# Modulation weights in four column pieces, gate products later, and 24 units of the second block's weights split on chip

## What is computed

```python
mod = silu(c) @ ada_w + ada_b                      # 6 x 1024 numbers, ada_w is 1024 x 6144
sh1, sc1, g1, sh2, sc2, g2 = split(mod)
h = rmsnorm(x, norm1_g) * (1 + sc1) + sh1
z, xbc, dt, u_v = split(h @ w_in)                  # w_in 1024 x 4624
xbc = silu(causal_conv4(xbc)); y = ssd_chunked(xbc, dt) + d * xs      # chunks of 128 tokens
y = group_rmsnorm(y * silu(z)); g = rmsnorm(u * spatial_gate(v))
x = x + g1 * (concat(y, g) @ w_out)
h = rmsnorm(x, norm2_g) * (1 + sc2) + sh2
x = x + g2 * ((silu(conv3(h @ w_up_gate)) * (h @ w_up_val)) @ w_down)
return rmsnorm(x, final_g)
```

## Time and profile before

| | |
|---|---|
| runs | 2772.1, 2769.61, 2765.91 us |
| the profiled execution's own time | 2763.87 us |
| its span | 2762.1 us |
| TensorE busy | 2697.5 us, 98% of the span |
| VectorE, ScalarE, GpSimd busy | 1815.1, 1003.4, 1072.4 us |
| DMA | 616.29 MB, mean 223 GB/s |
| granted TensorE clock | nine tenths or more in each of 40 slices |

### The profile page before, as it was taken

The page is one execution under the profiler, slowest core; times in us unless marked ns, Lnnn a source line. Parts: engine busy times, 40 slices in busy tenths (PEclk is TensorE's granted clock), DMA queues, the critical chain, the costliest instruction groups (busy, mean ns, idle before and its releaser), DMA issues.

```text
span 2762.1 us, 33801 instructions
## 1 busy us (share of the span) xinstructions
PE 2697.5 (98%) x12427; PEld 2207.2 (80%) x12427; DVE 1815.1 (66%) x2544; ACT 1003.4 (36%) x1521; POOL 1072.4 (39%) x739
## 2 busy tenths in 40 slices
PE   7999999999999999999999999999999999999998
PEld 6777887787878888887878888888888788887886
DVE  6977956768287565568787565555746855455767
ACT  3543325321153333343535322152223433334333
POOL 3444435445057777654650100001102544444240
PEclk9999999999999999999999999999999999999999
DMA  9876877999846566483448767587676334445646
GB/s 383 281 268 246 313 263 248 349 328 315 287 129 218 201 207 217 157 293 96 148 160 298 236 211 280 177 284 235 210 261 201 117 116 127 126 125 207 217 167 221
DMA packets 261872, 616.29 MB, mean 223 GB/s; under 512 B 26597, under 2 KB 84425, under 8 KB 257611
## 3 DMA queue, kind: packets, MB, share of 16 engines
q1 hardware_dynamic: 261046, 613.89, 64.9%
...
## 4 chain that ended last, share of the span: by engine, by line
PE 82%; DVE 6%; DMA 5%; issue 3%; POOL 2%; SPq 1%; ACT 1%; DVEq 0%; ACTq 0%; POOLq 0%
PE main L2038 34%; PE pair L2310 15%; PE main L2310 14%; PE pair L2330 6%; PE main L2330 5%; DMA w_split_scratch<-w_hl 2%; PE pair L2179 2%; POOL w_hl L739 1%; PE pair L2204 1%; PE pair L2164 1%; PE pair L2171 1%; DVE a_lo L1659 1%; DMA ada_t<-in_ada_w_dram 1%; DMA w_hl<-w_split_scratch 1%; POOL tb L750 1%
## 5 line engine op out<-in xcount | busy, mean ns | idle before, releaser
L739 POOL TENSOR_TENSOR w_hl<-w_raw,w_hl 128x512 fp32r<-128x512 f32 x548 | 794.2, 1455 | 920.5 <-ACT w_hl L844 918.8
L844 ACT ACTIVATE w_hl<-w_raw 128x512 fp32r<-128x512 f32 x548 | 342.3, 630 | 831.9 <-PE main L2310 169.4
L2038 PE MATMUL main<-w_hl,h_hi 128*128 128x512 f32 x1536 | 493.4, 403 | 5.1 <-DMA w_hl<-w_split_scratch 2.8
L2038 PEld LDWEIGHTS main<-w_hl,h_hi 128*128 128x128 f32 x1536 | 285.9, 189 | 77.8 <-issue 14.7
L2038 PE MATMUL main<-w_hl,h_lo 128*128 128x512 f32 x768 | 301.3, 392 | 0.0
L781 POOL TENSOR_TENSOR pre_hl<-pre_raw,pre_hl 128x512 fp32r<-128x512 f32 x35 | 51.0, 1461 | 566.3 <-ACT pre_hl L868 566.3
L2038 PE MATMUL main<-h_hi,w_hl 128*128 128x512 f32 x768 | 247.7, 396 | 7.4 <-POOL w_hl L739 4.2
L750 POOL TENSOR_TENSOR tb<-tb,tb 128x512 f32<-128x512 f32 x132 | 198.1, 1501 | 113.9 <-DMA tb<-in_ff_up_dram 109.5
L2310 PE MATMUL pair<-s_hi,w_hl 128*128 128x512 f32 x736 | 235.8, 393 | 2.4 <-POOL w_hl L739 2.4
L2330 PE MATMUL main<-w_hl,a_hi 128*128 128x512 f32 x704 | 219.2, 393 | 7.3 <-DVE a_lo L1659 3.9
L1659 DVE TENSOR_TENSOR a_lo<-g,a_hi 128x512 fp32r<-128x512 f32 x132 | 160.8, 1226 | 96.6 <-ACT a_hi L1094 96.1
...
## 6 DMA issues: line engine op xcount, KB each, us to landing
...
w_split_scratch<-w_hl SPq DMA_DIRECT2D x104, 512.0 KB, 7.1
...
```

Of the source, the lines that this page charges most:

```text
L739: nc.gpsimd.tensor_tensor(w_lo[:, g % RING, :], w_raw[:, g % RING, :], w_hi[:, g % RING, :].bitcast(F32), ALU.subtract).then_inc(w_lo_ok, 1)
L844: nc.scalar.activation(w_hi[:, g % RING, :], w_raw[:, g % RING, :], ACT.Copy).then_inc(w_hi_ok, 1)
L2038: ins = T.matmul(main[i], a, w, start=first and p == 0, stop=last and p == 2)
```

## The change

It has three parts.

First, the start. The first 2048 columns of ada_w are loaded as four pieces. Each has all 1024 rows and 256 columns of sh1 and the same 256 of sc1, and is loaded by four transfers of 128 x 4 x 256 elements, so each contiguous run is 1 KB where it was 8 KB (or 4 KB twice). `DIRECT` = (4, 4, 0, 0): of pieces 0 and 1 rows 0 to 511 go to TensorE, all others to VectorE as sums of 2 x 256 elements, 24 in all. A piece gives the modulation of two row tiles of h. The column products of pieces 1, 2 and 3 stand behind units 0, 2 and 4. The weights of units 0 to 7 stand between the pieces in SyncE's order. The x tiles for h use three banks, and four h_lo (`HF0` = 4) are done by GpSimd. VectorE scales two of the four x tiles.

Second, the gates. The tiles of ada_w for the gates are loaded at units 8, 10, 13, 15, 18, 21, 24 and 27 (`GATE_AT`), their sums are spread over the convolutions and chunk 0, and their products (now 4 x 512 into one bank) stand behind the scores of chunk 1. Ahead of the product with the state of chunk 1, TensorE waits for `gate_ok`, which the 4-row addition on VectorE sets. The loads for sh2 and sc2 move (`COL_AT`).

Third, block 1. `RAW_TO` goes from 20 to 28, so that eight more units are loaded raw and split. The steps of the sums 0, 1 and 2 alternate with the low parts of units 16 to 27. `T_AT` places the loads of sums 0, 1, 2 at units 16, 20, 24 and of the others from 28 on, so the store of sum t comes directly ahead of the load of sum t + 1 there.

```diff
-        ADA_RING, ADA_FIRST, HF0, ADA_PE = 12, 8, 2, 2
+        PIECES, HF0, ADA_SEMS, DIRECT = 4, 4, 12, (4, 4, 0, 0)
+        PW = D // PIECES
...
-        GATE_TILES = {8: 12, 11: 13, 14: 14, 17: 15}
-        COL_AT = {20: 1, 28: 0, 40: 2, 48: 3, 56: 4, 68: 5, 78: 6, 84: 7}
+        GATE_AT = {8: 0, 10: 1, 13: 2, 15: 3, 18: 4, 21: 5, 24: 6, 27: 7}
+        COL_AT = {31: 0, 41: 1, 43: 2, 48: 3, 56: 4, 68: 5, 78: 6, 84: 7}
...
-        T_AT = ((), [16 + 17 * i // 5 for i in range(20)], [18 + 19 * i // 2 for i in range(13)])
+        T_AT = ((), [16, 20, 24] + [28 + 33 * i // 10 for i in range(17)], [18 + 19 * i // 2 for i in range(13)])
...
-        RAW_FROM, RAW_TO = RING, 20
+        RAW_FROM, RAW_TO = RING, 28
...
+            def piece_load(p, half):
+                rows_h = ada_w[0, 4 * half * P:(4 * half + 4) * P, :].rearrange("(k p) (s d) -> p k s d", p=P, d=D)
+                for part in range(2):
+                    sp.dma_start(ada_p[p][:, 4 * half:4 * half + 4, part, :], rows_h[:, :, part, p * PW:(p + 1) * PW]
+                                 ).then_inc(ada_in[2 * p + half], 16)
...
-            first_step = RAW_TO - 4
+            first_step = RAW_TO - 12
             for n in range(RAW_FROM, RAW_TO):
                 if n >= first_step:
-                    t_step(0, n - first_step)
+                    t_step((n - first_step) // 4, (n - first_step) % 4)
                 low(mix0(1) + n)
-            for t in T_OF[1][1:]:
+            for t in T_OF[1][3:]:
                 for step in range(4):
                     t_step(t, step)
...
+            def piece_sum(p, k):
+                dve.wait_ge(ada_in[2 * p + k // 4], 32)
+                weighted(mod_sum[:, 0:2, p * PW:(p + 1) * PW], ada_p[p][:, k, :, :], k, k == DIRECT[p])
...
+                if b == 0:
+                    gate_sum(0)
...
-                        ada_sum(KD + 4)
+                        gate_sum(1)
...
-                        ada_sum(KD + 5)
-                        ada_sum(KD + 6)
+                        gate_sum(2)
+                        gate_sum(3)
...
-                        ada_sum(KD + 7)
+                        gate_sum(4)
...
-                        for m in range(4):
-                            dve.wait_ge(gate_mm, m + 1)
-                            row = gate_rows[0:1, m * W:(m + 1) * W]
-                            V.tensor_tensor(row, aux[m][0:1, :], row, ALU.add).then_inc(gate_ok, 1)
+                    if b == 0 and j == 2:
+                        gate_sum(5)
...
+                    if b == 0 and cc < NT - 1:
+                        if cc == 0:
+                            gate_sum(6)
+                        else:
+                            col_sum(2 * cc - 2)
...
+                    if b == 0 and cc == 1:
+                        dve.wait_ge(bias_in, 32)
+                        dve.wait_ge(gate_mm, 1)
+                        V.tensor_tensor(gate_rows[:], aux[3][0:4, :], gate_rows[:], ALU.add).then_inc(gate_ok, 1)
...
-                            col_sum(0)
-                        col_sum(cc + 1)
+                            gate_sum(7)
+                        else:
+                            col_sum(2 * cc - 1)
...
+                        if b == 0 and j == 0 and k in (0, 2, 4):
+                            piece_column(1 + k // 2, aux[3][:, 2 * KD:])
...
-                        if b == 0 and (j, k) == (2, 7):
-                            pe.wait_ge(ada_summed, GATES_SUMMED)
-                            pe.wait_ge(ws_ok, 2)
-                            pe.wait_ge(acs_t_ok, 1)
-                            for m in range(4):
-                                T.matmul(aux[m][0:1, :], ones, mod_sum[:, 2 + m // 2, (m % 2) * W:(m % 2 + 1) * W],
-                                         start=True, stop=True).then_inc(gate_mm, 1)
...
+                        if b == 0 and cc == 1 and k == 3:
+                            pe.wait_ge(ada_summed, GATES_SUMMED)
+                            for m in range(4):
+                                last = T.matmul(aux[3][0:4, :], pick[:, 3 - m:7 - m],
+                                                mod_sum[:, 2 + m // 2, (m % 2) * W:(m % 2 + 1) * W], start=m == 0, stop=m == 3)
+                            last.then_inc(gate_mm, 1)
                         if k == 5:
+                            if b == 0 and cc == 1:
+                                pe.wait_ge(gate_ok, 1)
                             chunk_yoff(cc)
```

More of the change, by code:

```diff
@@ L273, in hybrid_decoder_trunk @@
         const_ok, rows_in, small_in, pro_dma = sem("const_ok"), sem("rows_in"), sem("small_in"), sem("pro_dma")
-        ada_in = [sem(f"ada_in{i}") for i in range(ADA_RING)]
+        ada_in = [sem(f"ada_in{i}") for i in range(ADA_SEMS)]
         ada_summed, gate_mm = sem("ada_summed"), sem("gate_mm")
@@ L750, in t_step, with h_low0 @@
                 nc.gpsimd.tensor_tensor(dst, one, other, how).then_inc(t_add, 1)
-            for n in range(RING):
-                low(n)
-            for k in range(2, 2 + HF0):
+            def h_low0(k):
                 pool.wait_ge(h_hi_ok, k + 1)
@@ L828, in _ @@
             act.wait_ge(xr_ok, 1)
-            for t in range(NT):
-                tile = xn01[:, t, :] if t < 2 else xn23[:, t - 2, :]
+            for t in range(2):
+                tile = xn01[:, t, :]
                 nc.scalar.activation(tile, tile, ACT.Copy, scale=rstd[:, t:t + 1]).then_inc(xn_ok, 1)
```

242 lines of the change are left out of this document (131 added, 111 removed).

## The result

The changed kernel takes 2781.22 us (median of 6 runs, 2778.51 to 2787.11), the kernel before 2767.06 in the same count. The ratio is 1.0056, with a 95% interval of 1.0044 to 1.0068: 12 to 19 us slower. The forecast was 2780, from +10.8 us on the profiled execution. That execution now takes 2780.39 us, 16.5 more.

What follows compares the result with a forecast made beforehand. TensorE was taken as the bound, busy 2697.5 of 2762.1 us. Parts 1 and 2 (+2.1) and part 3 (+8.7) make +10.8 on 2763.87, so 2774.7; set on a median 5.7 above that execution: 2780, range 2765 to 2790.

Steps and rivals of the forecast that it cites:

- part 3: Mixer 1, units 20 to 28: eight more raw units and alternating steps make unit 28 begin 8.7 us later, 5.4 gained included.
- the turnaround: Mixer 1, GpSimd: 8.5 us from the last step of a sum to the next sum's first, 3.7 issue plus 4.8 landing.
- the prediction's own sign: Mixer 1: GpSimd idle for 8 us twice, ended by loads of tb; the prediction is wrong if those gaps are under 5.
- low half 24: Mixer 1: it waits for the tiles of sum 2 and ends at 491.8, where unit 24 began at 485.2: +6.6 us.
- part 1: Start, units 0 to 7 of mixer 0: unit 0 starts 9.3 us earlier, of which only 1.6 are left at unit 8.
- Rival 4: Start: the fourth weight still stands ahead of the first h_hi, unit 8 comes 1 us later, total 2783; chance 0.09.
- The price of the transfers: Start: a 2.1 MB piece of ada_w in 1 KB packets takes 7.3 us, between 5.1 and 7.9.
- Part 2: Gate sums and gate products, units 8 to 40 of mixer 0: together +3.7 us.
- xdec: Chunk 0: VectorE does gate sums 5 and 6 ahead of it; 1.1 to 3.2 us show, taken as +2.0.
- gate product: TensorE, behind the scores of chunk 1, where nothing hides it: +3.6 us.
- gate rows: Chunk 1, ahead of the product with the state: TensorE waits for VectorE's 4-row addition, 0 to 2.5 us, taken as +1.3.
- The product that went: Between units 23 and 24, TensorE's 3.59 us of gate products go; the third block's convolutions start 3.1 us earlier: -3.2.

## Why the prediction came out right, and where it didn't

**Right: part 3, the turnaround.** 8.5 us from the last step of a sum to the first of the next was the term that carried the forecast, and it measured 9.1, 8.2 and 8.0. The loss at units 20, 24 and 28 was forecast as 3.3, 6.6 and 8.7 us and measured 4.2, 7.8 and 8.6. Undoing the order took 7.6 of 9.5 us away at unit 28. That the last figure was hit to 0.1 us is luck in part: the waits came to 6.9 us net, with 2.60 at unit 28 for the 5 forecast, and 1.7 were half clock, which the sum didn't have. And the prediction's own sign, GpSimd's gaps of 8 us, not under 5, was badly chosen: a low half splits each turnaround, and the idle stretch ahead of the first step of sum 1 was 4.15. By its letter that sign spoke against a step that held.

**Right in size, wrong in who waits last: unit 24.** The step had TensorE waiting for low half 24. It waits for PSUM copies behind a split that waits for a raw weight; the low half came only 0.7 us earlier. The forecast named SyncE's weight behind the loads but didn't follow it into ScalarE's order. With the loads ahead of the stores, the stores' place is worth 3.9 us.

**Missing: half clock.** The waits after the change are 4.07 + 4.90 + 0.77 + 2.60 = 12.3 us, those that they replace 5.4. That is +6.9, and the place shows +10.4. Behind the waits of 4.07, 4.90 and 2.60 TensorE runs at 1.2 GHz for a while: of the seven stretches of 10 us from 460 to 530, one has a granted clock of 0.83 before (behind the wait of 2.82), and three have after. A clock of 0.83 over 10 us is 1.7 us of work, so two more such stretches make 3.4 of the missing 3.5. TensorE's busy time between the same two instructions bears it out: 73.85 us after, 70.42 before.

**Wrong: part 1, +4.1 at unit 8 for -1.6.** Unit 0 began at 31.07 for 30.1 forecast, and from there two steps failed. First, the sums were priced at 0.79 us each from L1379's median; they come every 0.86 us, and those beside GpSimd take twice as long, as the row's maximum of 1811 ns could have told. And VectorE begins them only behind the column arithmetic of the piece before. They ended at 58.1 for 54.2. Second, the column product of piece 3 stands behind unit 4, ahead of unit 5: unit 5, which doesn't need it, waits too, and runs at half clock. Rival 4, with unit 8 one us late and a total of 2783, lies as near to the measured total as the forecast does, but its reason isn't what happened: the fourth weight was split by 25.4, long before unit 0.

The price of the transfers was off the other way, with little consequence. From 12 to 20 us the queue moved:

```profile
q1 hardware_dynamic: 2613, 2.84, 109.4%
```

That is 355 GB/s, so 5.9 us for a piece, an estimate from this row, between the 5.1 of the 8 KB packets and the 7.3 taken. The Trainium skill's rule that transfers of 512 B and more go at line rate (DMA: Bandwidth & Descriptors, Specifications) is 14% too good here, and my fit to two mixed stretches 19% too bad (2613 x 0.026 + 2.84 x 34.9 = 167 engine-us for 140 used). With the pieces issued early the start gained 0.45 us.

**Part 2, +6.3 for +3.7: each term held, one was missing.** xdec 2.4 for 2.0, gate product 3.60, gate rows 1.5 for 1.3. The product that went gave 4.1 at once (from +6.0 to +1.9), of which 0.9 went into a longer wait at chunk 0, so 3.2 as in the forecast's sum (its text has 3.1 us). The 2.35 us at unit 16, for copies behind a split behind a store behind 1 MB of gate weights, were not seen. It is the same chain as at unit 24 of block 1.

**Missing: 4.5 us that come back.** Rows of the kernel before:

```profile
659.82 2.54 PE L2215 MATMUL pair<-ident,u_sb 128*128 128x128 f32 x14 [2.47 <-DVE u_sb L1533]
...
686.13 0.70 PE L2038 MATMUL main<-w_hl,gmT_hi 128*128 128x512 f32 x2 [1.83 <-DMA w_hl<-w_split_scratch]
```

After the change TensorE comes later and waits for neither. At the first it gets back 2.6 us, and 1.7 more because the stretch at half clock behind that wait goes too (+20.7 to +16.4). At the second it gets back 2.0 and loses 1.7 soon after, most of it in a new wait of 1.03 for y_sb at 707.58. The sum let every loss run to the end.

So the total came out nearer than its terms, and that is luck. Parts 1 and 2 were 8 us too low, part 3 was 2 too low at chunk 0, and 4.5 came back: 5.7 too low on the profiled execution. But the medians of six lie 14.2 us apart where the profiled executions lie 16.5, and the median that the sum was set upon (three runs, 2769.61) was 2.5 above that of six. That left 1 us. What the runs bear out is the mechanism of part 3 and, at its own place, its size; they don't bear out the split of the total.
